# A two-layer trunk on one core: the sample's first layer ahead of the prompt, and three tiles' second-layer inputs ahead of their stage

## The reference, cut to what matters

```python
h = rmsnorm(x, g_attn_norm) * (1 + sc1) + sh1
mix, new_ctx = branches(h, ...)          # three mixers and their merge, below
x = x + g1 * mix
h = rmsnorm(x, g_ffn_norm) * (1 + sc2) + sh2
x = x + g2 * peer(h, w_pq, keys, u_tab, v_tab)
...
# peer: for each token and each of 8 heads, the 16 best of 16384 experts
q = (hb @ w_pq).reshape(t, P_HEADS, 2, P_QDIM // 2)
sc = einsum('thpd,hpkd->thpk', q, keys)
sv, si = top_k(sc, 16)
cand = sv[:, :, 0, :, None] + sv[:, :, 1, None, :]
cv, ci = top_k(cand, 16);  eidx = ...;  gate = softmax(cv)
act = gelu(einsum('thkd,td->thk', u_tab[eidx], hb))
out = einsum('thk,thkd->td', gate * act, v_tab[eidx])
```

## Time and profile before

| | |
|---|---|
| median of 3 runs | 4987.1 us (4986.56 to 4990.98) |
| the profiled execution | 4990.76 us, of which 4989.0 us are the span that the profile covers |
| TensorE matmul busy | 3898.3 us (78%) |
| VectorE busy | 2904.0 us (58%) |
| ScalarE busy | 1629.8 us (33%) |
| GpSimd busy | 1576.1 us (32%) |
| moved by DMA | 1657.75 MB, 332 GB/s in the mean |
| the chain that ended last | PE 34%, DMA 31%, DVE 19%, issue 8% of the span |

### The profile page before, as it was taken

The page is one execution under the profiler, slowest core; times in us unless marked ns, Lnnn a source line. Parts: engine busy times, 40 slices in busy tenths (PEclk is TensorE's granted clock), DMA queues, the critical chain, the costliest instruction groups (busy, mean ns, idle before and its releaser), DMA issues.

```text
span 4989.0 us, 62323 instructions
## 1 busy us (share of the span) xinstructions
PE 3898.3 (78%) x20334; PEld 1598.2 (32%) x20334; DVE 2904.0 (58%) x6292; ACT 1629.8 (33%) x4847; POOL 1576.1 (32%) x1453
## 2 busy tenths in 40 slices
PE   5988899877887755778687689997788776666666
PEld 3555653332223311223223256333322232111111
DVE  3543444586667666676537643347756667766544
ACT  0211442223333323333423235222333333333333
POOL 0210002233343423445323210222334345444332
PEclk7999999988998977899798799998899998767666
DMA  7126039889999999999999520998899999999998
GB/s 290 49 99 229 3 121 399 349 333 370 421 421 401 420 407 420 368 393 397 375 421 397 207 74 1 366 380 322 331 416 421 396 421 416 421 421 421 421 421 352
DMA packets 238577, 1657.75 MB, mean 332 GB/s; under 512 B 27249, under 2 KB 31857, under 8 KB 42033
## 3 DMA queue, kind: packets, MB, share of 16 engines
q0 software_dynamic: 184320, 1342.26, 66.3%
q1 hardware_dynamic: 53936, 311.51, 16.1%
HBM read 1648.81 MB, written 4.85 MB: 331 GB/s over the span
## 4 chain that ended last, share of the span: by engine, by line
PE 34%; DMA 31%; DVE 19%; issue 8%; ACT 4%; DVEq 2%; SPq 1%; POOL 0%; ACTq 0%; POOLq 0%
DMA arena<-in_experts,arena 26%; PE ps L926 11%; PE ps L1183 10%; DVE sq L1686 8%; PE ps L1134 3%; PE ps L1159 3%; DMA arena<-in_weights 2%; PE ps L1147 2%; DMA front<-in_experts,arena 1%; DVE arena L1397 1%; ACT arena L1334 1%; PE ps L1062 1%; DVE arena L1400 1%; DVE arena L1395 1%; ACT arena L1330 1%
## 5 line engine op out<-in xcount | busy, mean ns | idle before, releaser
L1183 PE MATMUL ps<-arena 64*64 64x512 f32 x9264 | 1537.4, 744 | 793.2 <-ACT arena L1334 779.2
L899 POOL DMA_INDIRECT arena<-in_experts,arena x1158 | 1301.6, 1124 | 2515.2 <-PE ps L1183 2048.7
L1686 DVE CUSTOM_DVE_ANT_0 sq<-arena 128x1024 f32<-128x1024 f32 x1158 | 1420.9, 1227 | 866.1 <-DMA arena<-in_experts,arena 772.5
L1328 ACT ACTIVATE arena<-arena 128x1 f32<-128x1 f32 x1280 | 257.9, 201 | 2088.6 <-DVE arena L1686 2087.0
L1183 PEld LDWEIGHTS ps<-arena 64*64 64x64 f32 x9264 | 307.1, 151 | 1790.2 <-issue 1766.2
L926 PE MATMUL ps<-arena 128*128 128x512 f32 (+3 forms) x1920 | 835.8, 578 | 24.1 <-DMA arena<-in_weights 22.7
L1334 ACT ACTIVATE arena<-ident,arena 128x128 f32<-128x128 f32 x1280 | 513.8, 401 | 93.0 <-issue 5.2
L926 PEld LDWEIGHTS ps<-arena 128*128 128x128 f32 x1920 | 354.9, 196 | 502.1 <-issue 461.4
L1330 ACT ACTIVATE arena<-arena 128x1 f32<-128x1 f32 x1280 | 376.8, 294 | 89.1 <-issue 1.4
L1159 PE MATMUL ps<-arena 128*128 128x256 f32 (+1 forms) x1536 | 358.2, 377 | 9.6 <-DMA arena<-in_weights 5.2
L1159 PEld LDWEIGHTS ps<-arena 128*128 128x128 f32 x1536 | 257.1, 202 | 206.8 <-issue 177.7
(11 more groups left out here) (174 smaller groups left out, 3060.8 us busy)
## 6 DMA issues: line engine op xcount, KB each, us to landing
arena<-in_weights SPq DMA_DIRECT2D x249, 1024.0 KB, 9.1
arena<-in_experts,arena POOLq DMA_INDIRECT x1158, 14.3
arena<-mod_rows SPq DMA_DIRECT2D x26, 512.0 KB, 7.1
arena<-in_weights SPq DMA_DIRECT2D x12, 576.0 KB, 5.5
arena<-in_weights SPq DMA_DIRECT2D x6, 768.0 KB, 6.5
arena<-in_weights SPq DMA_DIRECT2D x9, 512.0 KB, 4.7
arena<-in_keysT SPq DMA_DIRECT2D x4, 1024.0 KB, 13.0
arena<-in_g_norm SPq DMA_DIRECT2D x7, 512.0 KB, 11.2
```

What stands on the lines that cost most here:

```text
L899: nc.gpsimd.indirect_dma_start(out=ring[BUF[n]], out_offset=None, in_=ins["experts"], in_offset=bass.IndirectOffsetOnAxis(ap=index(t)[:, s ...
L1183: last = MM(acc[h][to:to + 64, :], diag[n % 4][lo:lo + 64, lo:lo + 64], ring[BUF[n]][lo:lo + 64, D + c * 512:D + (c + 1) * 512], start=s = ...
L1328: A(gel[:, c:c + 1], dots[:, c:c + 1], ACT.Gelu_apprx_tanh)
L1686: V.tensor_tensor_reduce(out=sq[:], in0=ring[BUF[n]][:, 0:D], in1=h2_of_slot(n), scale=1.0, scalar=0.0, op0=ALU.mult, op1=ALU.add, accum_o ...
```

## The change

It puts the first layer of the sample tiles ahead of the prompt's. The lead now has the inputs of tiles 1 to 4 and the context, their attention, and `merge(0, 1)` with `route(0, 1, 1)`. The first stage has the 512 slots of layer 0's tiles 1 to 4; beneath them run `merge(0, 2)` and `route(0, 2)`, the choices, the modulation rows of layer 1, the whole first layer of the prompt up to its choice (inputs, attention, merge, route), and the second layer's inputs of tiles 1, 2 and 3. The middle has the inputs of tile 4 and the context, and the second attention. The second stage has 768 slots: the prompt's first layer, tiles 1 to 4 of the second layer, and the prompt's second layer, whose inputs, attention, merge, route and choice run beneath slots 330 to 560. Tile 0 gets a pass of its own over the input weights in both layers (`-4`), so that there are five passes where there were three. Gains are loaded a third time. Keys of three tiles are kept and fetched back. Scratch memory of tile 0 is moved, and the ring buffers get other limits. The long part of the diff that only renames helpers or renumbers waits is left out here.

```diff
-EARLY = (0, 1, 2)
-LATE = (3, 4)
+EARLY = (1, 2, 3)
+LATE = (4,)
...
-ETILES = [(l, t) for l in range(L) for t in range(NT)]
+ETILES = [(l, t) for l in range(L) for t in (1, 2, 3, 4, 0)]
+ORDER = {lt: e for e, lt in enumerate(ETILES)}
+STAGES = (0, NT - 1, len(ETILES))
...
 def schedule():
-    s = [("start",), ("consts", 0)] + mod_items(0, (0, 1))
-    s += with_mods(norm_and_inputs(0), mod_items(0, (2, 3, 4, 5)))
-    s += prompt_attention(0) + [("rows2", 0, 0), ("keys", 0, 0)]
-    s += merge(0, 0) + route(0, 0) + [("sink", 0)]
-    s += attention(0, (1, 2, 3, 4), choose(0, 0))
-    s += experts(0)
+    s = [("start",), ("consts", 0), ("scaled", 0)] + mod_items(0, (0, 1))
+    s += with_mods(norm_and_inputs(0, TILES[1:], CTX), mod_items(0, (2, 3, 4, 5)))
+    s += [("sink", 0)] + attention(0, TILES[1:])
+    s += [("rows2", 0, 1), ("keys", 0, 1), ("g2", 0, 1)]
+    s += merge(0, 1) + route(0, 1, 1)
+    line = Line()
+    line.slots(0)
+    line.spread(-4, 165, pieces(merge(0, 2) + route(0, 2)))
+    line.spread(12, 100, choose(0, 2))
+    line.spread(160, 215, mod_items(1))
+    line.spread(170, 235, choose(0, 3))
+    line.spread(205, 262, pieces(norm_and_inputs(0, (0,), ())))
+    line.spread(264, 280, prompt_attention(0) + [("rows2", 0, 0), ("consts", 1)])
+    line.put(292, [("scaled", 1)])
+    line.spread(282, 335, pieces(merge(0, 0) + route(0, 0)))
+    line.spread(262, 320, choose(0, 4))
+    line.spread(338, 385, choose(0, 0))
+    line.spread(390, 500, pieces(norm_and_inputs(1, EARLY, ())))
+    s += line.items()
     s += [("back", 1)] + norm_and_inputs(1, LATE, CTX)
-    s += [("sink", 1)] + attention(1, (1, 2, 3, 4))
-    return s + experts(1)
-
-
-def experts(l):
-
+    s += [("sink", 1)] + attention(1, TILES[1:])
+    s += [("rows2", 1, 1), ("keys", 1, 1), ("g2", 0, 0)]
     line = Line()
-    line.slots(l)
-    line.spread(-3, 118, pieces(merge(l, 1) + route(l, 1, 1)))
-    if l == 0:
-        line.spread(300, 384, mod_items(1))
-    line.spread(140, 236, choose(l, 2))
-    line.spread(118, 320, pieces(merge(l, 2) + route(l, 2)))
-    line.spread(322, 372, choose(l, 3))
-    line.spread(390, 490, choose(l, 4))
-    if l == 0:
-        line.put(334, [("consts", 1)])
-        line.spread(390, 520, pieces(norm_and_inputs(1, EARLY, ())))
-        line.spread(522, 545, prompt_attention(1) + [("rows2", 1, 0)])
-        line.spread(546, 605, pieces(merge(1, 0) + route(1, 0)))
-        line.spread(606, 638, choose(1, 0))
-    return [("rows2", l, 1), ("keys", l, 1), ("g2", l, 0)] + line.items()
+    line.slots(1)
+    line.spread(-3, 118, pieces(merge(1, 1) + route(1, 1, 1)))
+    line.spread(140, 236, choose(1, 2))
+    line.spread(118, 320, pieces(merge(1, 2) + route(1, 2)))
+    line.put(316, [("consts", 2)])
+    line.put(328, [("scaled", 2)])
+    line.spread(322, 372, choose(1, 3))
+    line.spread(330, 400, pieces(norm_and_inputs(1, (0,), ())))
+    line.spread(402, 420, prompt_attention(1) + [("rows2", 1, 0)])
+    line.spread(422, 490, pieces(merge(1, 0) + route(1, 0)))
+    line.spread(390, 460, choose(1, 4))
+    line.spread(500, 560, choose(1, 0))
+    return s + line.items()
...
 def first_pass(l, t):
 
-    return -2 if early(l, t) else -3
+    return -4 if t == 0 else -2 if early(l, t) else -3
...
-RELEASE = {6: lambda l: ("pq", l, 1, 15), 7: lambda l: ("pq", l, 2, 15), 8: lambda l: ("o", l, NT - 1, 1),
-           9: lambda l: ("sc", l, 2, 15), 10: lambda l: ("n2", l, NT - 1)}
-UNTIL = {4: 322, 6: 322, 7: 0, 9: 0, 10: 0}
+RELEASE = [{6: ("pq", 0, 1, 15), 8: ("o", 0, 4, 1)},
+           {6: ("pq", 1, 1, 15), 7: ("pq", 1, 0, 15), 8: ("o", 1, 4, 1), 9: ("n2", 1, 0), 10: ("sc", 1, 0, 15)}]
+UNTIL = [{4: 0, 6: 388, 7: 0, 9: 0, 10: 0}, {4: 306}]
...
-        keepa = {1: (17408, 15744), 2: (18432, 22528)}
-        keepc = {1: (12288, 12800), 2: (12544, 12928)}
+        keepa = {1: (17408, 15744), 2: (18432, 22528), 3: (HT0 + 4 * D - R0, 20992)}
+        keepc = {t: (12288 + 2 * P * (t - 1), 13056 + P * (t - 1)) for t in EARLY}
...
                 elif kind == "consts":
-                    if l:
-                        sp.wait_ge(slot_used, FINAL_IN[0, 4] + 1)
-                        sp.wait_ge(*ready("sink", 0))
-                        sp.dma_start(rope, ins["rope"]).then_inc(masks_in, 16)
-                    sp.dma_start(gains, to_all(row("gains", l))).then_inc(consts_in, 16)
-                    sp.dma_start(bs[:], row("b_s", l).rearrange("a p n -> (a p) n")).then_inc(consts_in, 16)
+                    if l == 1:
+                        sp.wait_ge(*ready("om", 0, 0, 1))
+                    elif l == 2:
+                        sp.wait_ge(slot_used, FINAL_IN[1, 4] + 1)
+                    sp.dma_start(gains, to_all(row("gains", min(l, 1)))).then_inc(consts_in, 16)
+                    sp.dma_start(bs[:], row("b_s", min(l, 1)).rearrange("a p n -> (a p) n")).then_inc(consts_in, 16)
...
                 elif kind == "rows1":
                     sp.wait_ge(mod_stored[0], 64 * (l + 1))
-                    if l and item[2] == 0:
-                        sp.wait_ge(*ready("n2", 0, NT - 1))
-                        sp.wait_ge(*full("sc", 0, LAST_GROUP, 15))
+                    t = item[2]
+                    if t == 0:
+                        sp.wait_ge(*ready("n2", l, NT - 1))
+                        sp.wait_ge(*full("sc", l, LAST_GROUP, 15))
+                    elif early(l, t):
+                        sp.wait_ge(*ready("n2", 0, 0))
+                        sp.wait_ge(*full("sc", 0, 0, 15))
                     elif l:
-                        sp.wait_ge(*ready("n2", 1, 0))
-                        sp.wait_ge(*full("sc", 1, 0, 15))
+                        sp.wait_ge(keysa_kept, 32 * len(EARLY))
+                        sp.wait_ge(keysc_kept, 32 * len(EARLY))
+                        sp.wait_ge(*ready("kcT", 1, EARLY[-1]))
+                        sp.wait_ge(*ready("qcN", 1, EARLY[-1]))
```

More of the change, by code:

```diff
@@ L197, in merge @@
     for j, t in enumerate(tiles):
-        s += [("o", l, t, 1), ("n2", l, t)] + ([("keys", l, 0)] if early(l, t) and gid == 0 else [])
+        s += [("o", l, t, 1), ("n2", l, t)] + ([("keys", l, 0)] if gid == 0 else [])
         s += [("hT2", l, tiles[j - 1])] if j else []
@@ L290, in spread, with slots @@
             self.points.append((a + (b - a) * at / total, i))
-    def slots(self, l):
-        n = l * NT * SLOTS
-        for s in range(NT * SLOTS):
+    def slots(self, stage):
+        tiles = ETILES[STAGES[stage]:STAGES[stage + 1]]
+        n = STAGES[stage] * SLOTS
+        for s in range(len(tiles) * SLOTS):
             self.put(s, [("E", n + s)])
@@ L297, in slots @@
             self.put(s + LAG, [("Emm", n + s)])
-        for t in range(NT):
-            end = (t + 1) * SLOTS - 1 + LAG
+        for i, (l, t) in enumerate(tiles):
+            end = (i + 1) * SLOTS - 1 + LAG
             self.put(end + .1, [("ea", l, t), ("ex", l, t)])
-            after = [("sw", l, t), ("ew", l, t)] + ([("g2", l, 1)] if t == 0 else []) + ([("y", t)] if l == L - 1 else [])
+            after = [("sw", l, t), ("ew", l, t)] + ([("y", t)] if l == L - 1 else [])
+            if (l, t) in ((0, 0), (1, 4)):
+                after += [("g2", 1, int(t == 0))]
             self.put(end + 2.1, after)
@@ L510 @@
 for _n in range(NSLOT):
-    _l, _s = divmod(_n, NT * SLOTS)
-    _there = [b for b in range(NBUF) if (_l or _s < UNTIL.get(b, NSLOT)) and (b not in RELEASE or (_s >= 6 and PLACE[RELEASE[b](_l)] < PLACE[("Emm", _n - 6)]))]
+    _g = stage_of(_n)
+    _s = _n - STAGES[_g] * SLOTS
+    _there = [b for b in range(NBUF) if _s < UNTIL[_g].get(b, NSLOT) and (b not in RELEASE[_g] or PLACE[RELEASE[_g][b]] < PLACE["Emm", max(_n - 6, STAGES[_g] * SLOTS)])]
     BUF.append(min(_there, key=lambda b: _last[b]))
@@ L605, in va @@
         def va(l, k, kept=True):
-            if early(l, k) and (k == 0 or not kept):
+            if k == 0 or early(l, k) and not kept:
                 return at(20992 if k == 0 else keepa[k][1], 512)
@@ L1146, in _ @@
                         w = weight(blocks[k // 4]).rearrange("p (k n) -> p k n", k=4)
-                        last = MM(dst, merged(l, t)[:, k * P:(k + 1) * P], w[:, k % 4, :], start=k == 0, stop=k == DK - 1)
+                        last = MM(dst, merged(t)[:, k * P:(k + 1) * P], w[:, k % 4, :], start=k == 0, stop=k == DK - 1)
                         halfway(item, k, last)
@@ L1163, in _ @@
                     if q == 0 and gid < 2:
-                        pe.wait_ge(keys_in, 16 * (2 * l + gid + 1))
+                        pe.wait_ge(keys_in, times(16, "keys", l, gid))
                     pe.wait_ge(*ready("pq", l, gid, q))
                     for j in range(len(GROUPS[gid])):
-                        last = MM(dst[:, j * P:(j + 1) * P], pqb(l, gid, q)[:, j * P:(j + 1) * P], keys[l][gid > 0][:, q, :], start=True, stop=True)
```

(13 more changed lines are left out.)

227 lines of the change are left out of this document (116 added, 111 removed).

## The result

The changed kernel takes 5021.49 us in the median (5009.74 to 5026.9, six runs); the kernel before, timed beside it, 4992.36 us (4986.56 to 4997.33, six runs). The ratio is 1.0058, 95% interval 1.0045 to 1.0072: slower by 0.6%, where 1.5% was forecast. The profiled execution has a span of 5018.8 us, 29.8 more than before.

The account below looks back on a forecast made before the run. The prediction took the slot stages as paced by transfers at 421 GB/s plus losses, and the lead and middle by TensorE. +55 - 38 + 64 - 9 = +72 us gave 5060 us, 1.5% slower; range for 8 in 10: 5005 to 5105.

Parts of the forecast that it names:

- What bounds the kernel: Both slot stages paced by transfers at 421 GB/s plus losses; the lead and middle limited by TensorE.
- The lead: Serial part before slot 0: pieces removed and added sum to +55 us, moving slot 0 from 723 to 778 us.
- The middle: Gap between the slot stages: one tile's inputs go, 44 us, less 6 us of new waiting: -38 us.
- Bytes: Beneath the slots of both stages: 27 MB more traffic, priced at 421 GB/s: +64 us.
- Rival 1: Slot stages: added bytes run within the 254 us of losses, which then sum under 175; 4979 us or less; chance 0.09.
- Losses: Slot-stage time lost by running below 421 GB/s: 108 us in the first, 137 in the second; 245 against 254, -9.
- The 25 us over tiles 3 and 4: First stage, their merge and route beneath slots with six, then seven buffers: loss taken between 8 and 67 us.
- The 31 us of early inputs: First stage: 31 us of loss charged for the second-layer inputs of three tiles beneath slots.
- 8 us of loss each: Tile 0's input pass in each slot stage: 8 us of loss charged besides its 12.85 MB of bytes.
- the term for fewer buffers: Second stage, slots 306 to about 490: seven buffers where eleven served, 8 us of loss.
- Rival 2: Too few buffers: the first-stage stretch of tiles 3 and 4 loses 14% instead of 5%, 60 us more; 5120 us; chance 0.13.
- Rival 3: Only the serial parts count, +55 - 38 = +17 us, all 64 us of bytes hidden; 4996 to 5005 us; chance 0.06.

## Why the prediction was wrong

**What bounds the kernel: right in the main.** Three runs price a MB at 1.9, 2.3 and 2.4 us, against 2.4 forecast; the added bytes show the full price, those left out four fifths of it. 1574 MB were moved, against 1575.

**The lead: right,** +56.6 for +55. Merge took 167 us for 169, route 119 for 118, the input pass 188 for 189, the attention 207 for 204. VectorE's turn and `top16` prices, counted with their drains, carried over.

**The middle: too much by 9 us,** -28.7 for -38. The pass lost 39 us of matmul time (98 to 59), not 44, and where I had taken 6 us of new waiting, TensorE's idle time in it rose by 10 (3 to 13), as the timeline's waits on VectorE show. About 4 of the 5 us of matmul time go with the lower granted clock behind these waits, 0.89 for 0.99; this is an estimate: the four groups behind the 5.7 us wait took 24.2 us, and would take 20.4 at the times per matmul that the same groups had in the kernel before. The other profiles with this middle are up to 7 us longer, so the saving was 22 to 29. A tile's price in a filled pass is not what the last but one tile gives back.

**Bytes: right,** +63 for +64 as traffic. Rival 1, that they fall into the gaps, came true in small part: its mark, losses under 175, was nearly reached (188), and the run with fewer bytes shows some 16 of the 61 us of the two passes covered in their own stretches. Added bytes were not covered at all, so it is refuted for the rest.

**Losses: this step failed,** "Sum 245 against 254: -9". Measured: 188 against 250, so -62. By stretch, forecast and measured:

| stretch | forecast | measured |
|---|---|---|
| tiles 3 and 4 beneath the first slots | 25 | 26.4 |
| modulation rows; tile 0's first inputs | 5 + 8 | 0.4 + 1.3 |
| its first attention, merge and route, choice | 13 + 6 + 5 | 10.5 + 5.3 + 6.3 |
| early inputs of three tiles | 31 | 19.5 |
| end of the first stage | 15 | 2.7 |
| second stage, slots 0 to 320 | 82 | 75 |
| prompt's second inputs, attention, merge and route | 8 + 13 + 6 | 4.4 + 16.1 + 1.2 |
| fewer buffers, slots 306 to 490 of the second stage | 8 | within the row above |
| end of the second stage | 20 | 18 |

The 25 us over tiles 3 and 4 came out to a us; it was picked between 8 and 67, so that is partly luck. The error is in the sum of the small ones, nearly all too high. Two have a shown cause. The 31 us of early inputs were read from a stretch that held a choice as well, which the change moves away: in the stretch from slot 390 on they lost 24, and putting a choice back raised this to 38. And for the two input passes of tile 0 I charged their bytes in full and 8 us of loss each beside them, where 1.3 and 4.4 came: without most of the bytes the losses of these stretches were 13 and 10, with them 1.5 and 5. Bytes and losses do not simply add there. At the end of the first stage, 4 of the 12 us come from another cut (148 for 152 before); that the rest of the old last stretch was the prompt's choice over six buffers, and that I charged both it and its end, was not tested. Nor was the term for fewer buffers: seven and ten run alike where nothing lies beneath, but the 8 us were for loaded slots that have seven in both runs. For the modulation rows, the second stage's first 320 slots and the remaining rows no run isolates a cause; they stay a mis-sized estimate, and why they came out low stays open.

**Rival 2, too few buffers,** did not come, but it was near: six for seven cost 11 us in the loaded middle, five for six 25 in the last 128 slots. **Rival 3,** the serial parts alone (4996 to 5005), lies nearer to 5021 than my 5060, and the two stages did take as long as before. But that is a balance of 63 us more of bytes and 62 less of losses, where it had all bytes hidden; only some 16 us of them were.

So the forecast of +72 stands against +30 by profile, because the losses fell by 62 us and not by 9: 31 us too much for the first stage's losses and 22 for the second's, 9 too little for the middle, and 1 or 2 for the rest.

## What to carry to other kernels

When a stage is paced by transfers, price added bytes at the measured ceiling, even where the stretch runs below it: an idle-looking tenth of the rate did not take them in. But do not charge a loss beside them as if they were not there: leaving them out gave back 38 of 54 us in their own stretches. A loss read from a stretch belongs to that mixture of work and number of buffers; when a change takes one of its parts away, take the loss apart first, or say only that it lies between zero and the old value. And a saving of serial lead is worth its length only net of what the idle transfers did meanwhile: 91 us of earlier start were worth 10.

## What the runs showed of the hardware

A gather took 20.2 us from issue to landing with ten buffers and 12.7 with seven, both at 421 GB/s, so at that rate the longer time is time in the queue. Adding traffic cost 2.3 to 2.4 us per MB, leaving 22.5 MB of weight loads out gave 1.9, and their stretches then ran at 393 and 402 GB/s, for 418 and 412. TensorE's clock in the one-tile pass of the middle was 0.89 of 2.4 GHz, with waits of 2.2, 5.7 and 2.7 us in it, and 0.99 in the two-tile pass, which was busy for 98 of 101 us.
